# First layer: the step sizes as grouped fp32 products outside the weight stream, eight more high parts on ScalarE

## The reference

```
h = rmsnorm(x, pre_norm[0])                       # x: 512 x 1024
z, xbc, dt = split(h @ w_in, [2048, 2048 + 4096]) # dt: 32 columns, one per head
xbc = silu(causal_depthwise_conv(xbc))            # 4 taps; then split into xs, B, C
dt  = softplus(dt + dt_bias)                      # the step sizes
A   = -exp(a_log)
y   = ssd_chunked(xs, dt, A, B, C) + d_skip * xs  # 4 chunks of 128 tokens, 8 groups of 4 heads
y   = rmsnorm(y * silu(z), gate_norm);  out = y @ w_out
```

## Time and profile before

| | us |
|---|---|
| median of 3 runs | 1847.44 (1846.95 to 1847.59) |
| the profiled execution | 1841.48 |
| its span, first to last instruction | 1839.7 |
| TensorE busy | 1812.5 (99%) |
| VectorE busy | 1086.6 (59%) |
| GpSimd busy | 893.3 (49%) |
| ScalarE busy | 548.6 (30%) |

### The profile page before, as it was taken

How to read it: one execution, slowest core, us unless ns; L and a number is a source line. 1 busy time by engine, 2 the same in 40 slices (tenths; PEclk the granted TensorE clock), 3 DMA queues, 4 the chain that set the end, 5 groups by cost and what they waited for, 6 DMA issues and landing times.

```text
span 1839.7 us, 24948 instructions
## 1 busy us (share of the span) xinstructions
PE 1812.5 (99%) x9675; PEld 1465.0 (80%) x9675; DVE 1086.6 (59%) x1663; ACT 548.6 (30%) x1016; POOL 893.3 (49%) x898
## 2 busy tenths in 40 slices
PE   8999999999999999999999999999999999999998
PEld 7888888788777787588888888888787788888887
DVE  7888888985887667653333313368989733333212
ACT  4544455413344330331111101236554211111001
POOL 5444444454533444255555555544433555555553
PEclk9999999999999999999999999999999999999999
DMA  8766676676754569488888878875653788888875
GB/s 250 168 153 162 145 157 158 153 171 146 171 116 103 129 158 245 119 187 192 195 193 191 190 188 198 200 172 138 138 127 79 175 190 195 197 191 191 187 166 135
DMA packets 92661, 309.15 MB, mean 168 GB/s; under 512 B 11136, under 2 KB 13312, under 8 KB 92544
## 3 DMA queue, kind: packets, MB, share of 16 engines
q0 software_dynamic: 42624, 147.87, 46.0%
q1 hardware_dynamic: 46752, 156.03, 24.9%
q10 hardware_dynamic: 3168, 3.65, 0.8%
HBM read 153.17 MB, written 2.10 MB: 84 GB/s over the span
## 4 chain that ended last, share of the span: by engine, by line
PE 87%; DVE 8%; issue 2%; ACT 1%; DMA 1%; POOL 0%; SPq 0%; DVEq 0%; ACTq 0%; POOLq 0%
PE gp L774 23%; PE gp L776 22%; PE gp L775 22%; PE gp L746 2%; PE gp L748 2%; PE gp L747 2%; PE gp L714 1%; PE gp L721 1%; PE gp L715 1%; PE mp L1035 1%; PE mp L1136 1%; PE mp L902 1%; PE mp L999 1%; PE mp L987 1%; DVE h_x L2519 1%
## 5 line engine op out<-in xcount | busy, mean ns | idle before, releaser
L656 POOL TENSOR_SCALAR wh<-stage 128x1024 fp32r<-128x1024 f32 (+3 forms) x296 | 349.4, 1180 | 823.2 <-PE gp L776 669.7
L774 PE MATMUL gp<-hh,wh 128*128 128x512 f32 x1504 | 598.8, 398 | 1.5 <-DMA wl<-stage 1.2
L775 PE MATMUL gp<-hh,wl 128*128 128x512 f32 x1504 | 585.7, 389 | 0.0
L776 PE MATMUL gp<-hl,wh 128*128 128x512 f32 x1472 | 574.0, 390 | 0.0
L662 POOL TENSOR_SCALAR wl<-stage 128x1024 fp32r<-128x1024 f32 (+3 forms) x296 | 350.8, 1185 | 0.0
L774 PEld LDWEIGHTS gp<-hh,wh 128*128 128x128 f32 x1504 | 282.3, 188 | 70.7 <-issue 14.1
L775 PEld LDWEIGHTS gp<-hh,wl 128*128 128x128 f32 x1504 | 282.6, 188 | 57.8 <-issue 1.4
L776 PEld LDWEIGHTS gp<-hl,wh 128*128 128x128 f32 x1472 | 276.3, 188 | 59.0
L665 POOL DMA_DIRECT2D wl<-stage x296 | 263.0, 888 | 94.1 <-POOL wl L662 84.9
L2446 DVE TENSOR_TENSOR val<-gp,rstd 128x512 f32<-128x512 f32 x44 | 30.4, 692 | 205.5 <-PE gp L776 205.5
L2306 DVE TENSOR_TENSOR xT<-gp,xT 128x512 f32<-128x512 f32 x31 | 21.4, 689 | 195.7 <-PE gp L776 189.8
(11 more groups left out here) (382 smaller groups left out, 2753.8 us busy)
## 6 DMA issues: line engine op xcount, KB each, us to landing
stage<-weights SPq DMA_DIRECT2D x263, 512.0 KB, 4.3
wl<-stage POOLq DMA_DIRECT2D x262, 512.0 KB, 5.3
stage<-weights SPq DMA_DIRECT2D x14, 384.0 KB, 3.4
wl<-stage POOLq DMA_DIRECT2D x14, 384.0 KB, 4.3
stage<-weights SPq DMA_DIRECT2D x19, 256.0 KB, 3.6
wl<-stage POOLq DMA_DIRECT2D x16, 256.0 KB, 3.3
c_s<-c_a ACTq DMA_DIRECT2D x40, 67.0 KB, 6.3
out<-rows_out SPq DMA_DIRECT2D x4, 512.0 KB, 3.2
```

Of the source, the lines that this page charges most:

```text
L656: pool.tensor_scalar(wh[:, s, part], stage[:, s, part], 1.0, 1.0, ALU.mult, ALU.mult).then_inc(hi_done, 1)
L774: pe.matmul(bank[:, :], wvh[:, cols], hi(kk), start=start, stop=False)
L775: pe.matmul(bank[:, :], wvl[:, cols], hi(kk), start=False, stop=False)
L776: mm = pe.matmul(bank[:, :], wvh[:, cols], lo(kk), start=False, stop=stop)
```

## The change

The 32 step-size columns leave the stream. They come as a tensor of their own (`dt_weights`, 128 KB), GpSimd scales them by the norm's weights, and TensorE multiplies them with x itself, all in fp32, right behind the lead: eight products with 32 columns, in four column groups of the array (step k goes to group k % 4), so that each group holds the sum of two steps (`group_dt`). VectorE multiplies by `rstd`; a second small product with the matrix `pick` adds the four groups up and spreads the chunks of tokens to 4 x 32 rows at once (`fold_dt`, behind the first granule of the unit B with C). `pick` holds 0.5, hence `scale=2.0` in ScalarE's reading. The first unit is now the first z tile of group 0; the third unit of group 0 has 128 columns. `turn_dt` and the `tokT` copy move from slots 5 and 4 of group 0 to slot 0 of group 1.

ScalarE makes the high parts of halves 4 to 11 too (`ACT_HALVES = 12`): two within the opening, two each in slots 1, 3 and 5 of group 0. GpSimd only negates and accumulates for these. SP waits for the high part of half q-4 before it reloads `stage` for halves 8 to 15. In the opening ScalarE's squares come two steps later than before and VectorE's additions two steps later. 17 warm-up products instead of 22. The first gate square is copied to `sqsum` instead of added to zeros.

```diff
@@ -71,6 +71,7 @@
 NEG = -1.0e30
 MAGIC = 1.5 * 2.0 ** 23
 N_PAR = 3
+ACT_HALVES = 12
 X_LOADS = ((0, 1), (1, 1), (2, 2), (4, 2), (6, 2))
 X_LOAD = [i for i, (_, n) in enumerate(X_LOADS) for _ in range(n)]
 EARLY = 2
...
@@ -172,11 +173,11 @@
         for n in range(6, 6 + 2 * i):
             add(f"down{i}", w["w2"][i], [(0, n * P, P)], [(0, 16), (16, 6)])
 
-    add("ssm", w["ssm_in"], [(0, SDT0, 32), (32, SDT0 - 96, 96)], whole)
+    add("ssm", w["ssm_in"], [(0, 0, P)], whole)
     for g in range(SG):
         add("ssm", w["ssm_in"], [(0, SI + g * UC, UC)], whole)
         add("ssm", w["ssm_in"], [(0, SB0 + g * P, P), (P, SC0 + g * P, P)], whole)
-        add("ssm", w["ssm_in"], [(0, g * UC, UC)], whole)
+        add("ssm", w["ssm_in"], [(0, g * UC, UC)] if g else [(0, P, P)], whole)
     out_proj("ssm_out", w["ssm_out"], [(0, 4), (4, 4), (8, 4), (12, 4)], [(0, 8), (8, 8)])
     for h in range(KVH):
         add("att", w["att_in"], [(0, h * UC, UC)], whole)
...
@@ -578,6 +587,7 @@
                 if q == HALVES:
                     load_x(3)
                     load_x(4)
+                    sp.dma_start(dtw[:, :, :], dt_weights.rearrange("p (k n) -> p k n", n=SH)).then_inc(dtw_landed, 16)
                 if q == HALVES + 2:
                     load_parameters(sp)
                 if q == place[phases["cp_out"][0] + 2, 0]:
...
@@ -596,6 +606,8 @@
                         sp.wait_ge(early_split, EARLY + s + 1)
                     else:
                         sp.wait_ge(lo_landed[s], 16 * (q // HALVES - 1))
+                        if q < HALVES + ACT_HALVES:
+                            sp.wait_ge(hi_done, q - HALVES + 1 - EARLY)
                 ka, kb = rows_of(u, i)
                 sp.dma_start(stage[:, s, 0:(kb - ka) * un.cols], packed(q)).then_inc(landed[s], 16)
             for c in range(NCH):
...
@@ -637,6 +649,11 @@
                 count[s] += 16
                 if q < EARLY:
                     continue
+                if q == HALVES + 2:
+                    pool.wait_ge(dtw_landed, 16)
+                    pool.wait_ge(pre_landed, 16)
+                    pool.tensor_tensor(dtw[:, :, :], dtw[:, :, :], prm[:, P_PRE:P_PRE + KT].unsqueeze(2).to_broadcast([P, KT, SH]),
+                                       ALU.mult).then_inc(dtw_scaled, 1)
                 pool.wait_ge(landed[s], count[s])
                 if q >= HALVES:
                     before, half = halves[q - HALVES]
...
@@ -652,9 +669,10 @@
                         pool.wait_ge(lv_read, 8 * HH)
                     if (u, i) == (phases["hg_out"][1] - 1, 0):
                         pool.wait_ge(split_done, split0["hg"] + KT)
-                if q >= HALVES:
+                if q >= ACT_HALVES:
+                    pool.wait_ge(hi_done, q - EARLY)
                     pool.tensor_scalar(wh[:, s, part], stage[:, s, part], 1.0, 1.0, ALU.mult, ALU.mult).then_inc(hi_done, 1)
-                else:
+                elif q < HALVES:
                     pool.wait_ge(hi_done, q + 1 - EARLY)
                     pool.tensor_tensor(wl[:, s, part], stage[:, s, part], wh[:, s, part].bitcast(F32),
                                        ALU.subtract).then_inc(early_split, 1)
...
@@ -826,12 +844,31 @@
                 keep_warm(8)
 
             pe.wait_ge(const_set, 1)
-            keep_warm(22)
+            keep_warm(17)
 
             def mamba():
+
+                def group_dt():
+
+                    pe.wait_ge(dtw_scaled, 1)
+                    for k in range(0, KT, NCH):
+                        for b in range(NCH):
+                            mm = pe.matmul(mp[1][b * SH:(b + 1) * SH, :], dtw[:, k + b, :], xT[:, k + b, :],
+                                           start=k == 0, stop=k + NCH == KT)
+                    mm.then_inc(dt_grouped, 1)
+
+                def fold_dt():
+
+                    pe.wait_ge(pick_made, 1)
+                    pe.wait_ge(dt_scaled, 1)
+                    for c in range(NCH):
+                        mm = pe.matmul(mp[2][c * SH:(c + 1) * SH, 0:P], pick[:, :].bitcast(F32),
+                                       dt_sum[:, c * P:(c + 1) * P], start=True, stop=True)
+                    mm.then_inc(dt_folded, 1)
 
                 gran = h_granules("ssm", "pre0", LEAD["ssm"], lambda: sum_squares(pre_round[0]), sum_early=True)
                 run(gran, 6)
+                group_dt()
                 pe.wait_ge(const_landed, 16)
 
                 def turn_dt():
...
@@ -912,11 +949,11 @@
                 for g in range(SG + 1):
                     def mix(slot):
                         if g == 0:
-                            if slot == 5:
-                                turn_dt()
                             return
                         p = g - 1
                         if slot == 0:
+                            if p == 0:
+                                turn_dt()
                             turn_x_b(p)
                             if p == 0:
                                 run(gran, 1)
...
@@ -936,7 +973,11 @@
                     if g == SG:
                         run(gran_out, 6)
                     for slot in range(6):
-                        if g < SG and (g or slot > 1):
+                        if g == 0 and slot == 2:
+                            run(gran, 1)
+                            fold_dt()
+                            run(gran, 1)
+                        elif g < SG and (g or slot in (3, 5)):
                             run(gran, 1 if (g, slot) == (1, 1) else 2)
                         mix(slot)
                         if g == SG:
...
@@ -1333,10 +1374,16 @@
             def later_high(q):
 
                 u, i = halves[q]
-                ka, kb = rows_of(u, i)
+                s, (ka, kb) = q % HALVES, rows_of(u, i)
                 part = slice(0, (kb - ka) * units[u].cols)
-                act.wait_ge(landed[q], 16)
-                act.activation(wh[:, q, part], stage[:, q, part], ACT.Copy).then_inc(hi_done, 1)
+                act.wait_ge(landed[s], 16 * (q // HALVES + 1))
+                if q >= HALVES:
+                    before, half = halves[q - HALVES]
+                    if half:
+                        act.wait_ge(gemm_part, unit_end[before])
+                    else:
+                        act.wait_ge(first_used, before + 1)
+                act.activation(wh[:, s, part], stage[:, s, part], ACT.Copy).then_inc(hi_done, 1)
 
             def pre_norm_of_x():
 
...
@@ -1344,13 +1391,19 @@
                     high_of_x(0, k)
                     if k == 0:
                         early_high(0, range(1, EARLY))
+                    elif k == 1:
+                        early_high(1)
+                    elif k == 2:
+                        later_high(2)
                     else:
-                        square(0, k - 1, xT[:, k - 1, :])
-                    if k == 1:
-                        early_high(1)
-                    elif k in (2, 3):
-                        later_high(k)
+                        square(0, k - 3, xT[:, k - 3, :])
+                    if k == 3:
+                        later_high(3)
+                square(0, KT - 3, xT[:, KT - 3, :])
+                later_high(4)
+                square(0, KT - 2, xT[:, KT - 2, :])
                 square(0, KT - 1, xT[:, KT - 1, :])
+                later_high(5)
                 take_rstd(0)
 
             def early_high(piece, which=range(EARLY)):
...
@@ -1392,8 +1445,8 @@
                 u, ab, e, w, lw = dtmp[0:5]
                 act.wait_ge(par_landed, 16 * N_PAR)
                 act.activation(hcol[:, 2:3], prm[:, P_ALOG:P_ALOG + 1], ACT.Exp).then_inc(dt_a, 1)
-                tile_taken(act, 0)
-                act.activation(u[:, :], u[:, :], ACT.Identity, bias=prm[:, P_DTB:P_DTB + 1]).then_inc(dt_read, 1)
+                act.wait_ge(dt_folded, 1)
+                act.activation(u[:, :], mp[2][:, 0:P], ACT.Identity, bias=prm[:, P_DTB:P_DTB + 1], scale=2.0).then_inc(dt_read, 1)
                 act.wait_ge(dt_read, 1)
                 step(act.activation(ab[:, :], u[:, :], ACT.Abs))
                 after()
...
@@ -1490,6 +1543,9 @@
                                 last_tap(g, slot)
                             if g == 0 and slot == 1:
                                 decay_rest()
+                            if g == 0 and slot in (1, 3):
+                                later_high(5 + slot)
+                                later_high(6 + slot)
                             if g == 0 and slot == 3:
                                 spread_decays()
                             if slot == 5 and g < SG - 1:
...
@@ -1517,6 +1573,9 @@
                                 silu(g, 2)
                         if g < SG and 2 <= slot < 4:
                             silu(g, slot - 2)
+                        if g == 0 and slot == 5:
+                            later_high(10)
+                            later_high(11)
                         if g == SG - 1 and slot == 5:
```

(58 more changed lines are left out.)

1 line of the change is left out of this document (removed).

## The result

Measured were 1848.27 us (median of 14 runs, 1845.97 to 1850.22) against 1844.58 us of the kernel before in the same comparison (14 runs, 1842.5 to 1847.59). The ratio is 1.0019, 95% interval 1.0012 to 1.0025: the change costs 3.5 us, and with that interval it is slower beyond doubt, though it lies just inside 0.2%. I had forecast 2.5 us less, and the median lies 0.3 us above my range. One of all the runs in this document, of the kernel of experiment 4 (2017.53 us at a mean granted clock of 0.847), was in a slow state and is left out of its ratio. The profiled execution took 1849.33 us, span 1847.5.

What follows compares the result with a forecast made beforehand. TensorE, busy 1812.5 of 1839.7 us, was taken as the bound. Terms -5.45 +2.0 +0.5 -1.5 +1.95 gave -2.5 us, applied to the median 1847.44: predicted 1844.9 us, range 1841.6 to 1848.0.

Steps and rivals of the forecast that it cites:

- The tile: Weight stream of group 0: one tile of 49 disappears with the padded step-size columns, -5.45 us.
- the grouped products: Right behind the lead: eight fp32 step-size products in four column groups, +2.0 us, bounds 1.8 and 6.9.
- the fold: Behind the first granule of B and C: four fp32 products plus shape change, +0.5 us (0.3 to 0.9), no wait.
- the token copy: Group 1, behind `turn_dt`: only two x transpositions stand between, so TensorE stalls 0.3 us.
- the wait for half 6: Ahead of the second z tile's first product: TensorE waits for ScalarE's high part, +1.45 us.
- VectorE's chain: Step-size operations behind the fold, ahead of ScalarE's decays: the last of five small operations ends at T1+11.4, with one block.
- T1: The start of the unit with B and C, behind the grouped products; the forecast's times in group 0 count from it.
- SP's waits: Stage loads of halves 10 to 15 move; half 10 lands about T1+17.5, its unit starts beyond T1+32; no stall counted.
- elsewhere in the first 100 us: Sign of being wrong: TensorE waits over a microsecond at a place not forecast, within the first 100 us.
- the clock: Wait ahead of the sum of squares: no cost counted; rival, a fall slows step 7 and grouped products, +4.1 us, chance 0.04.
- the opening: Ahead of the sum of squares: VectorE's last addition ends at 24.9 against 26.44, -1.5 us.
- clean-opening bound: Opening without collision or late square: the sum starts about 22, -4.5 us; rival with clean opening or small stall, chance 0.33.

Runs made afterwards that it cites:

- experiment 4: The changed kernel with ScalarE making only the high parts of halves 4 and 5, GpSimd those of 6 to 11; ratio 1.0025 to the kernel before.
- experiment 3: The kernel of experiment 2 with SP holding the stage load of half 10 and those behind it until the decays are done; ratio 1.0007 to the kernel before.
- experiment 5: The changed kernel with no high part of halves 4 to 11 on ScalarE; ratio 1.0040 to the kernel before.
- experiment 6: The kernel before with only ScalarE's high parts of halves 4 to 11, the new opening order and SP's waits; step sizes stay in the stream; ratio 0.9991.
- experiment 1: The changed kernel with twelve warm-up products of TensorE ahead of the sum of squares; ratio 0.9998 to the kernel before.
- experiment 2: The changed kernel with ScalarE making the high parts of halves 6 and 7 ahead of its wait for the folded step sizes; ratio 0.9996 to the kernel before.
- the best version: The changed kernel with twelve warm-up products, halves 6 and 7 ahead of ScalarE's wait, half 8 ahead of the decays, half 9 right behind; 1840.51 us, ratio 0.9976.
- experiment 9: The changed kernel once more, unaltered, to see whether the clock's falls recur; 1845.64 us in one run.

## Why the prediction was wrong

**What held.** The tile, the grouped products (1.85 of 2.0) and the fold (0.77 of 0.5) were sized rightly from rows of other stages, and the token copy too. The place and the cause of the wait for half 6 were right, its size (0.82 of 1.45) too large. VectorE's chain was timed well: I had its last operation end at T1+11.4, it ended at T1+11.55, with one collision among the five small operations, as I had assumed:

```profile
41.86 1.07 DVE L2005 SCALAR_TENSOR_TENSOR m_dt<-m_dt,m_dt 128x128 f32<-128x128 f32 x1
...
43.75 0.29 DVE L2011 TENSOR_SCALAR m_dt<-m_acs 128x128 f32<-128x128 f32 x1
```

The 1.07 at 41.86 is that one; the df operation, 2.80 in the earlier trace rows, took 0.29. The error is in what follows. ScalarE had the decays at 44.08, and halves 6 and 7, of 512 columns, took 0.57 each and not 1.04; I had used the row of a half twice as wide. The fold's 0.27 more took off the rest.

```profile
22.90 1.04 ACT L1386 ACTIVATE wh<-stage 128x1024 fp32r<-128x1024 f32 x1
...
44.08 0.31 ACT L1471 ACTIVATE m_dt<-m_dt 128x128 f32<-128x128 f32 x1 [2.90 <-DVE m_dt L2011]
44.29 1.13 ACT L1386 ACTIVATE wh<-stage 128x512 fp32r<-128x512 f32 x2
```

**Step that failed first: SP's waits.** I wrote that they "move the stage loads of halves 10 to 15" and checked each load only against its own unit ("half 10 lands about T1+17.5, and its unit starts beyond T1+32"). That was so. What I did not ask is what the late loads meet: half 8's and half 9's accumulations, issued at the same time, and wanted soon because the unit between has one tile only. GpSimd's side of half 9, the negation and the issue of the accumulation:

```profile
44.47 1.03 POOL L680 TENSOR_SCALAR wl<-stage 128x1024 fp32r<-128x1024 f32 x1 [0.50 <-PE gp L794]
45.80 0.89 POOL L683 DMA_DIRECT2D wl<-stage  x1 [0.30 <-POOL wl L680]
```

Issued at 45.80, it was there at 55.6. Experiment 3 shows the loads to be the cause, by putting them back alone: 2.0 us. In my sum this term was zero; it measured 2.41, and with the low clock behind it 3.98. It is the wait "elsewhere in the first 100 us" that I had named as a sign of being wrong. Two more of my figures were missed: the sum starts beyond 26, and the wait for ScalarE's high part of half 6 is under 1 us.

**Step that failed second: the clock.** This term too was zero in my sum: it measured 1.51 ahead of the sum, besides the 1.57 behind half 9. I had the rival (one wait of about 3 us ahead of the sum, price 4.1 us) and gave it 0.04, arguing that the clock was 1.00 in and behind a wait of 2.56 us. It was one row, of one execution. The fall came in two of three executions of the changed kernel ahead of the sum, and in all three behind the shorter wait for half 9. The price ahead of the sum was 1.5, less than I gave it, since the clock was back within step 7, after some 3.4 us; in experiments 4 and 5, where it stayed low for over 6 us, it was 2.8.

**Third, the opening: -0.3 us instead of -1.5.** I had VectorE through at 24.9, it was at 26.0. The work left at about 15.7 was as counted (6.2 us clean), but the collisions with GpSimd came to 3.4 us and not 2.4, and the last four additions, which wait for the squares behind ScalarE's high part of half 4 (22.90), lost 0.6 and not 0.3:

```profile
17.14 2.53 DVE L1884 SCALAR_TENSOR_TENSOR hl<-xT,prm,hh 128x512 fp32r<-128x512 f32 x1
...
20.63 1.10 DVE L1884 SCALAR_TENSOR_TENSOR hl<-xT,prm,hh 128x512 fp32r<-128x512 f32 x1
...
22.92 3.07 DVE L626 TENSOR_TENSOR sqsum<-sqsum,sq 128x512 f32<-128x512 f32 x4
```

```profile
17.78 1.35 POOL L680 TENSOR_SCALAR wl<-stage 128x1024 fp32r<-128x1024 f32 x1
...
20.04 1.14 POOL L655 TENSOR_TENSOR m_dtw<-m_dtw,prm 128x256 f32<-128x256 f32 x1
```

Low part 5, under the negation of half 5, took 2.53. The scaling of `dtw` held up an addition and a low part, 1.10 each. In experiment 6, which has the same order and no `dtw`, the two operations in their place took 0.74 and 0.68:

```profile
20.32 0.74 DVE L1847 SCALAR_TENSOR_TENSOR hl<-xT,prm,hh 128x512 fp32r<-128x512 f32 x1
```

The starts of the sum split the term: taking the high parts of halves 4 and 5 off GpSimd is worth 1.7 us (27.84 in experiment 5 against 26.13), as much as I forecast for the whole opening; without `dtw` it is 0.7 earlier (25.46 in experiment 6), and what is left, another 0.7, goes to the new order of squares and additions, which gathers the additions at the end. These are differences of single executions, and the nine with this opening start the sum between 25.76 and 26.34; the new order was not tried by itself. In the clean-opening bound, 15.73+4x2.04+0.25 should read 3x2.04: only three steps stand between, and the 22 is right for them.

**The number was nearer than the sum.** I applied my difference to 1847.44, the median of three runs. Over 14 runs before has 1844.58. The forecast of 1844.9 lies 3.4 us under the measured time, but the difference that it rested on was wrong by 6.2: the high median hid the rest.

With the clock held up, as in experiment 1, the ratio was 0.9998; with the loads in time, as in experiment 2, 0.9996. With both it was 0.9983, 3.1 us less: near the 2.5 that I had forecast without either, and not for my reasons: the opening still gave 0.2 us there, and half 8 cost 1.3.

## What to carry to other kernels

If a producer moves to another engine, its consumers' waits move too: follow each DMA that is now held back to what it will run beside, not only to its own deadline. Work in an in-order queue should stand ahead of a wait that it doesn't need, as halves 6 to 9 do in the best version. Two waits of 1 to 2.6 us drawn together into one of 3.4 can cost more than their sum, and a few idle products in it are a cheap insurance: with them the clock stayed up in all three executions traced, without them it fell in six of eight that had this wait.

## What the runs showed of the hardware

**The clock falls in some executions and not in others.** Ahead of the sum it fell to 0.50 behind waits of 2.7, 3.35, 3.4, 3.4, 3.7 and 4.2 us, and not behind 3.35 (experiment 3) and 3.7 us (experiment 9), nor behind the 2.6 for `hl` before the change. At the wait for half 9 it fell behind 2.0 to 2.2 us in four executions, and not behind 2.6 in experiment 1. The Trainium skill (TensorE: Matmul & The Clock Gate, "HAM oscillation — how this bites in real kernels") has idling between bursts as what takes the clock to half; the traces agree, but show that the length of a wait alone does not decide it.

**It is also the spread between runs.** Thirty runs of the kernel before range from 1842.46 us at a mean granted clock of 0.999 to 1847.79 at 0.994. One place of many is in the fourth layer, where both kernels have the same wait. After it the changed kernel (first row) ran at the low clock, the kernel before (second row) did not:

```profile
1391.38 1.09 PE L1206 MATMUL mp<-cst,h_vt 128*128 128x128 f32 x4 [2.41 <-DVE h_st L2637]
```

```profile
1387.23 0.63 PE L1165 MATMUL mp<-cst,h_vt 128*128 128x128 f32 x4 [2.42 <-DVE h_st L2580]
```

Of the twelve traces, that of before is the only one without such a fall between its mark and 1830 us. It took 1841.48 us, less than any of the 69 runs of before in the three larger comparisons, and I had taken the 6 us between it and the median of three for a constant offset.

**An accumulating DMA is slower beside loads.** A 512 KB accumulation into `wl` took 5.0 us from issue to landing with no stage load beside it, and 9.3 and 9.7 with two issued just ahead of it. The median of an issue group can hide this: for the changed kernel from 42 to 48 us the profile gives 7.4, the mean of half 8's 5.1 and half 9's 9.7.
